# Feed-forward weights read as 33 full slabs a block instead of 36 with quarter products at the start

## The reference

```python
def swiglu(x, w_gate, w_up, w_down):
    return (jax.nn.silu(x @ w_gate) * (x @ w_up)) @ w_down

def moe_ffn(x, w_router, w_gate, w_up, w_down):
    """Top-2-of-8 SwiGLU experts; token slots grouped by expert into 128-row blocks (no capacity limit)."""
    ...
    def run(args):
        xb, e = args
        return swiglu(xb, w_gate[e], w_up[e], w_down[e])
    yp = lax.map(run, (xp.reshape(n_blocks, MOE_BLOCK, D), block_e)).reshape(P, D)
    ...

    for layer in range(DEPTH):
        x = x + hybrid_mixer(...)
        h = rms_norm(x, norm_ffn[layer])
        if layer % 2 == 0:
            x = x + swiglu(h, w_dense_gate[i], w_dense_up[i], w_dense_down[i])
        else:
            x = x + moe_ffn(h, w_router[i], w_moe_gate[i], w_moe_up[i], w_moe_down[i])
```

## Time and profile before

| What | us |
|---|---|
| median of three executions | 1365.21 |
| the profiled execution's own time | 1367.71 |
| its span, first to last instruction | 1365.9 |
| TensorE busy | 1313.0 (96%) |
| VectorE busy | 1143.1 (84%) |
| ScalarE busy | 877.3 (64%) |
| the 383 `w_lo` instructions of VectorE | 794.6 |
| the 383 `w_hi` instructions of ScalarE | 669.9 |

### The profile page before, as it was taken

One profiled execution on the slowest core, in us unless ns is written; L12 is line 12 of the kernel. 1 busy time (PEld: TensorE's weight loads), 2 busy tenths in 40 slices (PEclk: granted clock), 3 DMA queues, 4 the chain that ended last, 5 costly groups with the idle time before them and its releaser, 6 DMA issues.

```text
span 1365.9 us, 17429 instructions
## 1 busy us (share of the span) xinstructions
PE 1313.0 (96%) x6156; PEld 984.7 (72%) x6156; DVE 1143.1 (84%) x1233; ACT 877.3 (64%) x964; POOL 79.8 (6%) x61
## 2 busy tenths in 40 slices
PE   6999999999999999999999998999999999999998
PEld 5787778888887887788666776666766667666675
DVE  6988987654448889885998988999889998899998
ACT  3445555444435445645777777987779877798775
POOL 0011001000000110100060000000000000000400
PEclk9999999999999999999999999999999999999999
DMA  8343343965493435152999999999999999999996
GB/s 338 139 179 133 121 168 132 392 244 184 154 361 124 151 127 185 63 201 77 393 363 374 419 340 373 410 401 421 389 363 404 396 423 379 364 412 393 421 387 263
DMA packets 63316, 394.75 MB, mean 289 GB/s; under 512 B 6641, under 2 KB 7233, under 8 KB 23570
## 3 DMA queue, kind: packets, MB, share of 16 engines
q1 hardware_dynamic: 58610, 375.41, 70.8%
q10 hardware_dynamic: 2848, 11.53, 2.1%
q0 software_dynamic: 1792, 6.95, 1.4%
HBM read 376.44 MB, written 17.43 MB: 288 GB/s over the span
## 4 chain that ended last, share of the span: by engine, by line
PE 62%; DVE 19%; issue 5%; ACT 4%; DMA 1%; DVEq 0%; POOL 0%; ACTq 0%; SPq 0%
DVE w_lo L1193 13%; PE bank L2077 13%; PE bank L1775 13%; PE bank L1776 13%; PE bank L2054 9%; PE bank L1825 4%; ACT w_hi L793 3%; DVE ys L1182 1%; PE bank L1920 1%; PE bank L1788 1%; PE bank L2064 1%; PE bank L1820 1%; PE bank L2171 1%; DMA raw<-in_moe 1%; DVE act L1587 1%
## 5 line engine op out<-in xcount | busy, mean ns | idle before, releaser
L1193 DVE TENSOR_TENSOR w_lo<-raw,w_hi 128x2048 fp32r<-128x2048 f32 (+2 forms) x383 | 794.6, 2089 | 94.6 <-ACT w_hi L793 93.3
L793 ACT ACTIVATE w_hi<-raw 128x2048 fp32r<-128x2048 f32 (+2 forms) x383 | 669.9, 1755 | 133.1 <-PE bank L2077 55.3
L1775 PE MATMUL bank<-w_hi,hT_hi 128*128 128x512 f32 (+3 forms) x968 | 382.9, 396 | 2.7 <-DVE hT_lo L1182 1.6
L1776 PE MATMUL bank<-w_hi,hT_lo 128*128 128x512 f32 (+3 forms) x968 | 375.2, 388 | 0.0
L1775 PEld LDWEIGHTS bank<-w_hi,hT_hi 128*128 128x128 f32 (+1 forms) x968 | 170.2, 176 | 52.1 <-issue 5.2
L1776 PEld LDWEIGHTS bank<-w_hi,hT_lo 128*128 128x128 f32 (+1 forms) x968 | 170.3, 176 | 44.7 <-issue 1.0
L2054 PE MATMUL bank<-w_lo,hT_hi 128*96 128x512 f32 (+3 forms) x616 | 162.3, 387 | 0.8 <-DVE w_lo L1193 0.8
L2054 PEld LDWEIGHTS bank<-w_lo,hT_hi 128*96 128x96 f32 (+1 forms) x616 | 103.1, 169 | 37.3 <-DVE w_lo L1193 4.3
L1825 PE MATMUL bank<-w_lo,hT_hi 128*128 128x512 f32 x352 | 87.8, 392 | 0.6 <-DVE w_lo L1193 0.3
L2139 PE MATMUL bank<-w_lo,hT_hi 128*128 128x512 f32 (+1 forms) x264 | 78.2, 414 | 9.7 <-DVE w_lo L1193 9.6
L1006 ACT ACTIVATE act_hi<-bank 128x192 fp32r<-128x192 f32 (+1 forms) x66 | 24.7, 374 | 92.3 <-PE bank L2064 92.3
(11 more groups left out here) (280 smaller groups left out, 1348.7 us busy)
## 6 DMA issues: line engine op xcount, KB each, us to landing
raw<-in_moe SPq DMA_DIRECT2D x240, 1024.0 KB, 7.9
raw<-in_mix SPq DMA_DIRECT2D x56, 1024.0 KB, 4.9
raw<-in_dense SPq DMA_DIRECT2D x30, 1024.0 KB, 4.9
raw<-in_moe SPq DMA_DIRECT2D x16, 768.0 KB, 8.4
raw<-in_moe SPq DMA_DIRECT2D x12, 512.0 KB, 7.5
slot_h<-x_squared ACTq DMA_DIRECT2D x1, 5632.0 KB, 43.4
slot_y<-x_squared ACTq DMA_DIRECT2D x1, 5632.0 KB, 24.3
raw<-in_moe SPq DMA_DIRECT2D x8, 256.0 KB, 5.1
```

Source lines behind the costliest of these rows:

```text
L793: nc.scalar.activation(HI[:, split_slot, 0:width], RAW[:, raw_slot, half:half + width], ACT.Copy)\
L1193: vec.tensor_tensor(LO[:, split_slot, 0:width], RAW[:, raw_slot, half:half + width], HI[:, split_slot, 0:width].bitcast(F32), ALU.subtract ...
L1775: mm(out_, left[0], right[0], start=start, stop=False)
L1776: mm(out_, left[1], right[1], start=False, stop=False)
```

## The change

Every feed-forward block has 33 slabs in 33 places of the ring. The four quarter slabs are two full ones, and the last two down slabs are one of 1536 columns: the first 1024 are what slab 34 was, the last 512 what slab 35 was. The slabs keep their names p = 4 to 34; the first two are now p = 2 and 3 (`FFN_FIRST`), and p = 35 and 36 are the first two of the next block (`FFN_END` is 35). The two are issued as full slabs, each by its own DMA. What follows:

- ScalarE and VectorE split one full slab where they split one quarter (before the tokens of the next block), and one where they split the second and third. The split of the fourth quarter, at the head of a block, is gone.
- TensorE works through the first chunk in two products of four k-tiles each instead of four products of two, with the same matmuls in all. `add_y_lo` comes after the first of two (it came after the second of four). In layer 0 the two transposes `turn_h(0, 2)` and `turn_h(0, 3)` come between the high and the low matmuls of the first product.
- Block 0 of layer 1 takes its dummy output after slab 4 instead of before.
- The last block skips three places, not two: p = 19 to 21 take over the raw buffer of the slab three before, p = 22 to 24 that of nine before, each in two DMAs.

The diff, cut to its core (index arithmetic and the host's copy of the layout left out):

```diff
-FFN_SLABS = 36
+FFN_SLABS = 33
+FFN_FIRST = 2
+FFN_END = FFN_FIRST + FFN_SLABS
...
-FFN_PLACES = FFN_SLABS - 2
-LATE_SLAB = 19
-REJOINED = (LATE_SLAB - 2 + RAW_SLOTS, LATE_SLAB - 1 + RAW_SLOTS)
+LATE_SLAB, LATE_SKIP = 19, 3
+LATE_PLACES = FFN_SLABS + LATE_SKIP
+REJOINED = range(LATE_SLAB + LATE_SKIP, LATE_SLAB + 2 * LATE_SKIP)
 def ffn_place(p, late=False):
 
-    return p // 2 if p < 4 else p if late else p - 2
+    return p - FFN_FIRST + (LATE_SKIP if late else 0)
...
-FFN_WIDTHS = [4 * CHUNK] * 4 + [SLAB] * 27 + [8 * TAIL] * 2 + [SLAB, D, D // 2]
+FFN_WIDTHS = [SLAB] * 29 + [8 * TAIL] * 2 + [SLAB, D + D // 2]
...
 def back(p, late=False):
 
-    place = ffn_place(p, late)
-    if place < RAW_SLOTS:
-        return p + RAW_SLOTS - place
-    place -= 2 * RAW_SLOTS if late and p in REJOINED else RAW_SLOTS
-    return p - (2 * place + 1 if place < 2 else place if late and place >= LATE_SLAB else place + 2)
+    if late and p in REJOINED:
+        return RAW_SLOTS + LATE_SKIP
+    return RAW_SLOTS - LATE_SKIP if late and p < LATE_SLAB + LATE_SKIP else RAW_SLOTS
...
the SyncE block:
-                for p in (0, 2):
-                    two_halves(e, at, p, n0 + p)
+                for p in (FFN_FIRST, FFN_FIRST + 1):
+                    slab(e, at, p, n0 + p, False)
...
-                for p in range(28, FFN_SLABS):
+                for p in range(28, FFN_END):
...
the ScalarE block:
                     squares(2 * tb + half, "norm_ffn")
                 if half == 0:
                     split_to(first + 1, stage)
-                elif layer == 0:
-                    split_to(first + 2, stage)
             turned_h(2)
             turned_h(3)
             if layer == 0:
 
                 a.do(nc.scalar.activation(SQUARES[:, 0:1], HALF[:, 0:1], ACT.Silu))
             if layer == 1:
-                split_to(first + 2, stage)
 
...
-                ffn_split(3, b, n0, r0, 4 * CHUNK)
-                act.wait_ge(slab_used, n0)
+                act.wait_ge(slab_used, n0 + FFN_FIRST)
                 take_y(l)
                 ffn_split(4, b, n0, r0)
...
-                ffn_split(34, b, n0, r0, D)
+                ffn_split(34, b, n0, r0, D + D // 2)
                 lo_copy(n0 + 32, 0, TAIL)
                 silu_light(qb + NCH, k0 + NCH, 0, TAIL)
-                ffn_split(35, b, n0, r0, D // 2)
                 turned_hi_light(qb + NCH)
                 turned_tokens_hi(b + 1, CAP)
-                ffn_split(FFN_SLABS, b, n0, r0, 4 * CHUNK)
-                ffn_split(FFN_SLABS + 1, b, n0, r0, 4 * CHUNK)
-                act.wait_ge(slab_used, n0 + FFN_SLABS)
+                ffn_split(FFN_END, b, n0, r0)
+                act.wait_ge(slab_used, n0 + FFN_END)
                 nc.scalar.activation(R["y_lo"][P - LCAP:P, 0:512], PS[4][P - LCAP:P, :], ACT.Copy).then_inc(sem("y_lo_ready"), 1)
-                ffn_split(FFN_SLABS + 2, b, n0, r0, 4 * CHUNK)
+                ffn_split(FFN_END + 1, b, n0, r0)
...
-                ffn_split(3, at, n0, r0, 4 * CHUNK)
-                if is_moe:
-                    if y_added is None:
-                        act.wait_ge(slab_used, n0)
-                    else:
-                        act.wait_ge(sem("y_lo_added"), y_added)
+                if y_added is not None:
+                    act.wait_ge(sem("y_lo_added"), y_added)
                     take_y_light(y_added)
                 ffn_split(4, at, n0, r0)
+                if is_moe and y_added is None:
+                    act.wait_ge(slab_used, n0 + FFN_FIRST + 1)
+                    take_y_light(y_added)
                 ffn_split(5, at, n0, r0)
...
                 turned_hi(qb + NCH - 1, 1)
-                ffn_split(34, at, n0, r0, D)
+                ffn_split(34, at, n0, r0, D + D // 2)
                 silu(qb + NCH, n0 + 32, 0, TAIL)
-                ffn_split(35, at, n0, r0, D // 2)
                 turned_hi(qb + NCH, 0)
                 if is_moe:
-                    ffn_split(FFN_SLABS, at, n0, r0, 4 * CHUNK)
+                    ffn_split(FFN_END, at, n0, r0)
                     turned_tokens_hi(b + 1, CAP if spread or y_added is None else LCAP)
...
-                        act.wait_ge(slab_used, n0 + FFN_SLABS)
+                        act.wait_ge(slab_used, n0 + FFN_END)
                         nc.scalar.activation(R["y_spread"][0:CAP, 0:512], PS[4][0:CAP, :], ACT.Copy)\
                             .then_inc(sem("y_spread0"), 1)
-                    ffn_split(FFN_SLABS + 1, at, n0, r0, 4 * CHUNK)
-                    ffn_split(FFN_SLABS + 2, at, n0, r0, 4 * CHUNK)
+                    ffn_split(FFN_END + 1, at, n0, r0)
...
the VectorE block:
-                        split_to(FIRST["ffn", layer] + 1, ("ffn", layer))
+                        split_to(FIRST["ffn", layer], ("ffn", layer))
...
-            if layer == 0:
-                split_to(first + 2, stage)
             turned_h(2)
             turned_h(3)
+            if layer == 0:
+                split_to(first + 1, stage)
...
-                ffn_split(3, b, n0, 4 * CHUNK)
-                dve.wait_ge(slab_used, n0)
+                dve.wait_ge(slab_used, n0 + FFN_FIRST)
                 take_y(l)
                 ffn_split(4, b, n0)
...
                 mult_light(qb + NCH, 0, TAIL)
-                ffn_split(34, b, n0, D)
+                ffn_split(34, b, n0, D + D // 2)
                 turned_lo_light(qb + NCH)
-                ffn_split(35, b, n0, D // 2)
                 turned_tokens_lo(b + 1, CAP)
-                ffn_split(FFN_SLABS, b, n0, 4 * CHUNK)
-                ffn_split(FFN_SLABS + 1, b, n0, 4 * CHUNK)
-                dve.wait_ge(slab_used, n0 + FFN_SLABS)
+                ffn_split(FFN_END, b, n0)
+                dve.wait_ge(slab_used, n0 + FFN_END)
                 vec.tensor_copy(R["y_lo"][P - LCAP:P, 512:1024], PS[5][P - LCAP:P, :]).then_inc(sem("y_lo_ready"), 1)
-                ffn_split(FFN_SLABS + 2, b, n0, 4 * CHUNK)
+                ffn_split(FFN_END + 1, b, n0)
...
+                if y_added is not None:
+                    dve.wait_ge(sem("y_lo_added"), y_added)
                     take_y_light(y_added)
                 ffn_split(4, at, n0)
+                if is_moe and y_added is None:
+                    dve.wait_ge(slab_used, n0 + FFN_FIRST + 1)
+                    take_y_light(y_added)
...
-                    ffn_split(FFN_SLABS, at, n0, 4 * CHUNK)
+                    ffn_split(FFN_END, at, n0)
                     if spread:
-                        dve.wait_ge(slab_used, n0 + FFN_SLABS)
+                        dve.wait_ge(slab_used, n0 + FFN_END)
                         vec.tensor_copy(R["y_spread"][0:CAP, 512:1024], PS[5][0:CAP, :]).then_inc(sem("y_spread1"), 1)
                     turned_tokens_lo(b + 1, CAP if spread or y_added is None else LCAP)
...
the TensorE block:
-            def down_last(n, s, q):
+            def down_end(n, s, q):
 
                 def term(left, right, last=False):
 
+                    for tb in range(tbs):
+                        tok = slice(tb * rows, (tb + 1) * rows)
+                        for half in range(2):
+                            mm(PS[4 + 2 * tb + half][0:rows, :], left[:, 0, tok], right[:, s, half * 512:half * 512 + 512],
+                               start=False, stop=False)
                     for tb in range(tbs):
                         tok = slice(tb * rows, (tb + 1) * rows)
                         for half in range(2):
                             part = slice(half * P // 2, half * P // 2 + P // 2)
-                            ins = mm(PS[4 + 2 * tb + half][0:rows, :], left[part, 1, tok], right[part, s, 0:D // 2],
+                            ins = mm(PS[4 + 2 * tb + half][0:rows, :], left[part, 1, tok], right[part, s, D:D + D // 2],
                                      start=False, stop=last)
                     return ins
...
+                def turn_rest():
+
+                    turn_h(0, 2)
+                    turn_h(0, 3)
+
+                for part in range(2):
+                    if is_moe:
+                        pe.wait_ge(g_lo_ready, 2 * b + part + 1)
+                    gate_up(n0 + FFN_FIRST + part, slot(FFN_FIRST + part), 4 * part, 4, CHUNK, qb, 0, None if is_moe else "fht",
+                            None if is_moe or part else turn_rest)
+                    if part == 0 and y_ready is not None:
                         add_y_lo(y_ready)
-                    if part == 0 and not is_moe:
-                        turn_h(0, 2)
-                        turn_h(0, 3)
...
-                down(n0 + 34, slot(34), q + 1, False, tiles=((0, P),))
-                down_last(n0 + 35, slot(35), q + 1)
+                down_end(n0 + 34, slot(34), q + 1)
```

135 lines of the change are left out of this document (60 added, 75 removed).

## The result

The changed kernel took 1377.34 us (median of three, 1375.82 to 1377.63), the kernel before 1365.21: a ratio of 1.0082, 95% interval 1.0066 to 1.0099. Five more executions, in a later set, gave 1377.34 again, with 1.0087 (1.0072 to 1.0102). Its profiled execution took 1375.82 us, with a span of 1374.0.

A forecast was written before the change was run, and what follows sets the result against it. TensorE was taken to bound heavy blocks and VectorE light ones, with loads nearly a bound. Terms 1.9 + 3.9 + 2.4 + 1.6 + 0.2 - 1.0 = +9.0 us on the median 1365.2 gave 1374.2 us, range 1368 to 1380.

The forecast's parts named there:

- a longer last split: End of light blocks: VectorE's split of 1536 columns takes 0.53 us longer, so TensorE ends the block 0.5 later.
- the first full slab: Start of heavy blocks after light ones: TensorE waits 0.4 us more for the low part of the first full slab.
- the end: End of the kernel: the wider split pushes VectorE's last output copy by about 1.2 us, all but 0.2 hidden.
- Heavy to heavy, 1.9: Seam from block 0 to 1, once: tokens come 1.93 us later behind the full slab, nothing covers it; 1.9 taken.
- Heavy to light, TensorE 1.9 later and 1.3 for slab 5: Three seams: late tokens start TensorE 1.9 us later, and VectorE's work from slab 5 on 1.3 later; 3.9 in all.
- Light to heavy, 0.8: Three seams: longer last split and wait for the first full slab, less 0.1 given back, cost 0.8 us each; 2.4.
- Last block, 1.6: Last block's raw buffers: with distance three, slab 21 loads late and its low activations come 1.7 us late; 1.6 taken.
- Loads regained, -1.0: Light blocks 4 and 6: a later start gives loads time, so half the 1.1 us waits in each is saved; -1.0.
- Layer 0 and the start of block 0, 0: TensorE has 2.8 us of matmuls in hand to cover a full slab's 2.285 us low part; 0, bounds -0.5 and +0.5.
- the lead decides: Rival: more VectorE work done early at light blocks' heads, plus joined instructions, gives -4.1 us, 1361; faster had chance 0.06.
- TensorE's matmuls are the same in number and shape: Premise on the cost of the split: TensorE's matmuls stay the same in number and shape; no term in the sum.
- The rival of more drops: Rival: longer idle at seams drops TensorE's clock at three more seams, 1.5 us each, giving 1378.7; chance 0.17.

The follow-up runs named there:

- e1: The changed kernel with the tokens' copies ahead of the full split at the end of heavy blocks 0, 1, 3 and 5, on ScalarE and VectorE; 1373.59 us.
- e2: The changed kernel with VectorE's 1536-column split in light blocks made in two instructions, the low part of the last activations between them; 1376.58 us.
- e6: The changed kernel with the first two slabs of blocks 1 to 7 as halves in the old order, and 128-row products before 64-row ones at the last slab; 1366.60 us.
- e5: The changed kernel with TensorE's products at the joined last slab grouped, all of 128 rows first, then all of 64; 1379.59 us.
- e3: The changed kernel with the last block's three skipped places of the raw-buffer ring ahead of slab 13 instead of 19; 1379.37 us.
- e10: The changed kernel with two unused 256-column matmuls ahead of TensorE's wait for tokens at the start of blocks 1, 2, 4 and 6; 1378.08 us.
- e12: The kernel of e6 with ScalarE copying slab 5 ahead of its `add_lo` copy at the start of light blocks; 1364.95 us.
- e11: The changed kernel with the first two slabs as halves only at light to heavy seams (blocks 3, 5 and 7); 1375.66 us.

## Why the prediction was right, and where it was not

The direction held, and 1377.3 lies in the range, 3.1 above the forecast. The main mechanism was right: late tokens at heavy to light seams, a late light block on VectorE, a longer last split. The sum was partly helped by luck: two terms had the right size by parts that were wrong in opposite ways, and the order of TensorE's products and the clock, worth about 4 us together, were not in it. Against that stand terms that were too large (the first full slab, the last block, the end) and a gain that it did not have (block 0), about 3.3 us together.

*Heavy to heavy, 1.9.* Right. The pause grew by 1.53 - 0.31 = 1.2 us, and block 0 ends about 0.65 later by the alternation. The tokens stand where the prediction put them, 1.9 later. TensorE's later end is covered by the wait for them, so it does not come on top.

*Heavy to light, TensorE 1.9 later and 1.3 for slab 5.* Right in both numbers: block 3 is 1.94 us longer (95.31 - 93.37), and in block 4 the products run 1.94 - 0.71 = 1.2 later from slab 5 on. In block 2 slab 5's copy comes at 838.96 for 836.22, 2.7 later, of which 1.5 was lost before the seam, where block 1 had its stretch at half clock. But "the tokens come late" was only half the cause. By e1, with the tokens early, the heavy to light pair gains next to nothing, since two full low parts end no sooner.

*Light to heavy, 0.8.* Right in size, 0.9, and by luck. The longer last split (0.5) is there: the last slab's first product comes 0.52 later after the products before it. The term for the first full slab (0.4) was mis-sized, 0.03 against the kernel before. In its place stands the order of the products, 0.38, which the prediction did not have. The first full slab is not free for all that: in e2 its copy becomes what TensorE waits for as soon as the split is shortened.

*Last block, 1.6.* The mis-sized term: 0.3 in the changed kernel's first profile and 0.5 in its second. The chain itself was right, 5.1 us from slab 18's split to slab 21's copy where the prediction had 4.9, and 1.3 for the addition. (Its landing at 1315.7 is 0.2 more than 1310.63 + 4.9; without a source for the 0.2 its own terms make 1.5 late, not 1.7.) But slab 18 was split 1.4 us sooner against TensorE's work than before: in the kernel before the loads of slabs 16 and 17 came late, and VectorE idled ahead of both for them (its timeline, behind ScalarE's copies), here less so (0.59 and 0.20). That this lead is why the term came out small is argued, not shown by an experiment.

```profile
1302.08 2.29 DVE L1193 TENSOR_TENSOR w_lo<-raw,w_hi 128x2048 fp32r<-128x2048 f32 x1 [1.06 <-ACT w_hi L793]
...
1305.76 2.29 DVE L1193 TENSOR_TENSOR w_lo<-raw,w_hi 128x2048 fp32r<-128x2048 f32 x1 [1.06 <-ACT w_hi L793]
```

The estimate by the Trainium skill ("DMA: Bandwidth & Descriptors", the part on the anatomy of one DMA), 4.4 us a load, would have been further off than the row's 4.9. The Trainium skill gives that fit for transfers that GpSimd issues, and these are issued by SyncE.

*Loads regained, -1.0.* Right: ScalarE waits for no load in block 4 any more, where it waited 1.1 us, and 0.4 instead of 1.2 in block 6. TensorE wins back 0.49 us in block 4 (in its products between 1071 and 1079 us) and 0.54 in block 6.

*Layer 0 and the start of block 0, 0.* Right only in the sum. TensorE loses 0.85 us at the end of layer 0 by the new order, and wins 0.8 in the first 35 us of block 0, where VectorE also computes where tokens go: eight profiles of changed kernels, matched with the kernel before, all have that gain between its 645 and 680 us. It looks like the lead of the rival "the lead decides" (0.9), at a block start that does not stand behind late tokens, but no experiment isolates it.

*"TensorE's matmuls are the same in number and shape".* True and not enough, for their order changed. This is the missing cost: 0.85 us in layer 0, 0.64 at each heavy block's end, 0.38 at each light one's, 2.9 us where TensorE's path runs through them (e6). In the changed kernel the pause for tokens covers the heavy blocks' part (e5), except in the last block, where its 0.64 stands in place of the prediction's 0.2 for the end.

*The clock.* The rival of more drops asked for three more seams at 1.5 us. Its price was right (mostly 1.3 to 1.6 us for a stretch), its number was not: the fit gives 1.4 us in all. From block 1 to the last microseconds the drops come in two places, with two exceptions (in e3 and e5): right at the seam from 0 to 1 (in four of seven profiles with a pause there, in none of the seven without), and 10 to 14 us into a light block, which is not "just after the waits of that seam" and which filling the seam's pause (e10) does not touch. TensorE has two or three waits of 0.4 to 1.6 us in the first 13 us of every light block, in the kernel before too, and in 22 of the 42 light blocks profiled the clock falls at one of them or shortly after. What makes it fall in one and not in the next stays open.

The sum of what is measured: 0.85 (layer 0) - 0.8 (block 0) + 1.9 + 3 x 1.2 + 3 x 0.9 - 1.0 + 0.4 (last block) + 0.6 (order at the end) = 8.3, with the clock 9.7, of about 11.5. The remaining 1.8 us is no more than the half width of the interval, 2 us, and I have no cause for it.

## What to carry to other kernels

At a seam between two stages the grain counts, not the total: a joined instruction saves 0.16 us and delays whatever is queued behind it, and whatever needs its first half, by 0.9 to 1.1. When two pieces of unlike shape are joined, write down the new order on the consumer too; the same matmuls in alternating heights took 0.64 us more. And an engine's wait can stand behind a small instruction that waits for something else: moving one copy ahead of it (e12) was worth 0.5 us in each light block. Last, two changes that hide each other, like the longer split and the first full slab's copy, give nothing back when only one is undone (e2, e11); match two traces product by product before calling either of them free.

## What the runs showed of the hardware

A change between products of 128 and of 64 rows of weights costs TensorE 0.16 to 0.21 us each time, by the difference between the alternating and the grouped order; grouped, pairs of 64-row products start 0.24 to 0.30 us apart and 128-row ones 0.47 to 0.56. Executions of one kernel differ by up to 8.6 us, and the granted clock explains a bit under half of the variance, 0.62 us for each us of full clock lost. A stretch of 3.4 us at half clock, 1.7 us of full clock lost, mostly costs 1.3 to 1.6 us where it falls into an expert block, about the 1.5 that the prediction took; the fit's mean over all places, 1.1, is lower.
